# A hybrid encoder block on one core: attention's and gates' units as one matmul of 512 columns, evacuated by two engines

## The chip, the cores and the metric
The kernel runs on one core of a Trainium2 chip. The metric is the time of one execution on the device in microseconds; the median of three runs before the change is 1985.73 us (1985.63 to 1985.82).

## The reference, cut to what matters
One encoder layer on 256 tokens of width 2048, all in fp32:
```
xn   = rms_norm(x) * gain
cols = xn @ w_in      # q (16 heads of 128) | k, v (4 heads) | RWKV-7 columns | gate_attn | gate_rwkv
q, k = rope(q), rope(k)
o_attn = softmax(q k^T / sqrt(128), window 128, with a sink logit) @ v
merged = sigmoid(gate_attn) * o_attn + sigmoid(gate_rwkv) * o_rwkv
h = x + rms_norm(merged @ w_out)
h = h + rms_norm(relu(rms_norm(h) @ w_ffn_up)^2 @ w_ffn_down)
```
The change touches the projection of q, k, v and gate_attn alone.

## The kernel before
**Units.** Every weight matrix is streamed through SBUF in units of 1 MB: a unit is a block of 128 columns of w_in by all 2048 rows, as 16 tiles (k) of 128 x 128. SyncE loads it to a slot of `raw`. ScalarE rounds it to fp32r (`whi`, the high part), VectorE computes the rest (`wlo` = raw - whi). Tokens are held in the same way, turned: xT[:, k, 0, :] is high, xT[:, k, 1, :] low. whi and wlo have two buffers each and the banks PB[0] and PB[1] alternate by unit. A unit's product is high x high + high x low + low x high.

In `unit_b` this is three matmuls of 256 columns for each k, into columns 0 to 255 of the bank (lines 1586 to 1588). `unit_wide`, which the up projection of the feed-forward part uses (lines 1600 and 1602), and `dense` in the pair stage (lines 1766 and 1768) move the high and the low tokens together as 512 columns under the high weights, and then the high tokens under the low weights into columns 0 to 255; the result is the sum of the bank's two halves.

**Stages.** Units 0 to 23 are attention's: for each of four groups g a key, a value and four query units (steps j = 0 to 5). Units 24 to 39 are gates' (four, then a loop of three times four). Then come the RWKV-7 pairs, the output projection and the feed-forward part, to the end.

**Order by hand.** Each engine walks through the steps with its own `step` function, in a written order, and waits on semaphores. The four heads of group g are handled one step after another, shifted: within step j, the scores of head h have j = h + 3, the turn of its probabilities (transposes, line 1663) j = h + 4, and the product with the values (`weigh`, line 1672) j = h + 5, all modulo 6. So it is in every engine:
- TensorE, step of unit u: wait that unit u - 2 is evacuated (`d_evac`) and that this unit's low part is there (`w_lo`); the first four k, `weigh`, four more k; `scores` (line 1654, waits for the rotated query `q_r`); the last eight k (`w_used`); `turn` (waits for the normalised probabilities `prn`).
- ScalarE: `evacuate` after `w_used` (lines 493 to 495: the tokens, and the tokens with halves of 64 partitions exchanged, for the rotation; line 485 for values), the copy of an attention output to mrg (512), the copy of the turned probabilities to prT (507), the high part of unit u + 2 (477), the exponentials (521, wait for `neg`). For a gate, `gate_tanh` (502) from the bank takes the place of `evacuate`.
- VectorE: `maxima` (950 to 959, wait for `sc`), `rotate` (930, 931, 937, wait for `d_evac`) or, for a gate, `gate_product` (944), the low part of unit u + 2 (976; 872 in the gates' loop), `normalise` (964 to 969, wait for `ex`).

SyncE starts a load of attention when the low part of the unit three places earlier has been computed, in the gates with four slots.

## Time and profile before
| | |
|---|---|
| median of three runs | 1985.73 us |
| the profiled execution's own time | 1988.33 us |
| its span, first to last instruction | 1986.5 us |
| mean granted TensorE clock | 0.997 |
| TensorE busy | 1931.3 us |
| VectorE, ScalarE, GpSimd busy | 1357.8, 941.9, 379.1 us |
| bytes by DMA | 281.24 MB, 142 GB/s |

A row of a view in order of time has start and busy time in us, engine, line, operation, tiles written and read, and in brackets the idle time before it and what ended it. PE is TensorE's matmuls, PEld its weight loads, DVE VectorE, ACT ScalarE, POOL GpSimd. The ends of matmuls are modelled. A wait is put down to the signal that came last.

### The profile page before, as it was taken

The page shows a single profiled execution, that of the slowest core. Times are in us where ns is not written, and L with a number is a line of the kernel's source. Part 1 is how long each engine was busy: PE and PEld are TensorE (multiplying, and loading weights), DVE is VectorE, ACT ScalarE, POOL GpSimd, SP SyncE. Part 2 cuts the span into 40 slices and gives each one's busy share as a digit, 9 for nine tenths or more (in the row PEclk, how much of TensorE's full clock was granted, in tenths as well). Part 3 has the DMA queues.
Part 4 walks back from the last instruction along what each step waited for, and adds up shares of the span by engine and source line. Part 5 has one row for each costly group of instructions (what it writes and reads, how often), then busy time and mean ns, then how long its engine had stood idle before and what let it go on. Part 6 is the DMA issues. An engine that isn't in the chain of part 4 may idle for free.

```text
span 1986.5 us, 35360 instructions
## 1 busy us (share of the span) xinstructions
PE 1931.3 (97%) x12443; PEld 1720.7 (87%) x12443; DVE 1357.8 (68%) x2357; ACT 941.9 (47%) x1669; POOL 379.1 (19%) x451
## 2 busy tenths in 40 slices
PE   6999999999999999999999999999999999999997
PEld 6999999888888888888888888888888888888886
DVE  4666546888888888888888864656565655556565
ACT  5555434455454555545555544544443434444443
POOL 1000000444343333434344531100000000000001
PEclk9999999999999999999999999999999999999999
DMA  7455676433333333333331426456666665666663
GB/s 224 135 140 148 172 189 159 131 92 91 91 82 78 85 91 91 91 91 91 81 80 48 134 85 241 120 191 191 191 190 191 189 190 191 189 192 188 195 186 126
DMA packets 415373, 281.24 MB, mean 142 GB/s; under 512 B 14074, under 2 KB 372700, under 8 KB 414556
## 3 DMA queue, kind: packets, MB, share of 16 engines
q1 hardware_dynamic: 414908, 277.43, 48.3%
q10 hardware_dynamic: 416, 3.15, 0.4%
q8 instruction: 32, 0.52, 0.1%
q14 instruction: 17, 0.14, 0.0%
HBM read 278.46 MB, written 2.10 MB: 141 GB/s over the span
## 4 chain that ended last, share of the span: by engine, by line
PE 73%; issue 10%; DVE 9%; POOL 6%; ACT 1%; DMA 0%; DVEq 0%; POOLq 0%; SPq 0%; ACTq 0%
PE bank L1600 12%; PE bank L1602 6%; PE bank L1766 6%; PE bank L1616 6%; PE bank L1617 6%; PE bank L1618 6%; PE bank L1586 4%; PE bank L1588 4%; PE bank L1587 4%; POOL CT L1513 3%; DVE wlo L872 3%; PE bank L1768 3%; PE bank L1895 2%; PE bank L1913 1%; PE bank L1745 1%
## 5 line engine op out<-in xcount | busy, mean ns | idle before, releaser
L1766 PE MATMUL bank<-xT,whi 128*128 128x512 f32 x1024 | 318.0, 418 | 0.0
L872 DVE TENSOR_TENSOR wlo<-raw,whi 128x1024 fp32r<-128x1024 f32 (+2 forms) x181 | 259.1, 1438 | 47.7 <-ACT whi L449 43.6
L1403 DVE TENSOR_TENSOR wlo<-raw,whi 128x1024 fp32r<-128x1024 f32 x126 | 154.4, 1225 | 163.0 <-ACT whi L834 158.8
L1600 PE MATMUL bank<-xT,whi 128*128 128x512 f32 x1024 | 245.7, 391 | 0.0
L834 ACT ACTIVATE whi<-raw 128x1024 fp32r<-128x1024 f32 x126 | 133.1, 1056 | 206.1 <-PE bank L1618 206.1
L1600 PEld LDWEIGHTS bank<-xT,whi 128*128 128x128 f32 x1024 | 188.1, 188 | 36.2
L1586 PE MATMUL bank<-xT,whi 128*128 128x256 f32 x736 | 216.6, 294 | 0.6 <-DVE wlo L872 0.6
L1588 PE MATMUL bank<-xT,wlo 128*128 128x256 f32 x736 | 207.9, 283 | 0.0
L1587 PE MATMUL bank<-xT,whi 128*128 128x256 f32 x736 | 207.9, 283 | 0.0
L1616 PE MATMUL bank<-whi,ft 128*128 128x512 f32 x512 | 199.3, 389 | 0.0
L1617 PE MATMUL bank<-wlo,ft 128*128 128x512 f32 x512 | 199.3, 389 | 0.0
L1618 PE MATMUL bank<-whi,ft 128*128 128x512 f32 x512 | 199.2, 389 | 0.0
L441 ACT ACTIVATE whi<-raw 128x1024 fp32r<-128x1024 f32 x190 | 198.9, 1047 | 0.0
L1768 PEld LDWEIGHTS bank<-xT,wlo 128*128 128x128 f32 x1024 | 167.3, 188 | 28.8
L1766 PEld LDWEIGHTS bank<-xT,whi 128*128 128x128 f32 x1024 | 171.2, 191 | 16.8 <-issue 0.3
L1768 PE MATMUL bank<-xT,wlo 128*128 128x256 f32 x1024 | 176.0, 280 | 0.0
L1513 POOL TENSOR_TENSOR CT<-G,lmk 128x256 fp32r<-128x256 f32 x192 | 145.0, 760 | 75.6 <-PE bank L1895 74.3
L1410 DVE TENSOR_TENSOR wlo<-raw,whi 128x1024 fp32r<-128x1024 f32 x126 | 153.5, 1218 | 0.0
L1570 POOL TENSOR_TENSOR acc<-acc,gain 128x512 f32<-128x512 f32 x6 | 8.8, 1487 | 703.0 <-ACT junk L818 703.0
L1586 PEld LDWEIGHTS bank<-xT,whi 128*128 128x128 f32 x736 | 140.7, 191 | 1.6 <-issue 0.7
L1587 PEld LDWEIGHTS bank<-xT,whi 128*128 128x128 f32 x736 | 140.8, 191 | 0.9
L1588 PEld LDWEIGHTS bank<-xT,wlo 128*128 128x128 f32 x736 | 140.7, 191 | 0.0
(234 smaller groups left out, 3833.2 us busy)
## 6 DMA issues: line engine op xcount, KB each, us to landing
raw<-in_w_in SPq DMA_DIRECT2D x106, 1024.0 KB, 6.0
raw<-in_w_ffn_up SPq DMA_DIRECT2D x64, 1024.0 KB, 6.4
raw<-in_w_ffn_down SPq DMA_DIRECT2D x64, 1024.0 KB, 5.0
raw<-in_w_out SPq DMA_DIRECT2D x16, 1024.0 KB, 5.6
raw<-in_w_in SPq DMA_DIRECT2D x4, 768.0 KB, 4.6
xtok<-in_x SPq DMA_DIRECT2D x2, 1024.0 KB, 6.1
upg<-in_g_up SPq DMA_DIRECT2D x16, 128.0 KB, 3.4
hres<-in_x ACTq DMA_DIRECT2D x1, 2048.0 KB, 10.8
```

Source lines behind the costliest of these rows:

```text
L441: A.activation(whi[:, u_static % 2, 1024:], raw[:, u_static % 4, 1024:], ACT.Copy).then_inc(w_hi.sem, 1)
L872: x = V.tensor_tensor(wlo[:, u_static % 2, part], raw[:, u_static % 4, part], whi[:, u_static % 2, part].bitcast(f32), ALU.subtract)
L1513: Gp.tensor_tensor(in_blocks(CT[c][:].rearrange("p a b -> p (a b)"), l), woven(G[:, 0, :, :, :], l, 2 * c, 2), in_blocks(lmk[:, l, :, :].r ...
L1586: M(bank[:, 0:T], h, xT[:, k, 0, :], start=k == 0, stop=False)
L1587: M(bank[:, 0:T], h, xT[:, k, 1, :], start=False, stop=False)
L1588: x = M(bank[:, 0:T], l, xT[:, k, 0, :], start=False, stop=k == KT - 1)
L1600: M(bank[:, :], hi[:, P * k:P * k + P], xT[:, k, :, :], start=k == 0, stop=False)
L1616: M(banks[b][:, :], ah, wh, start=f, stop=False)
L1617: M(banks[b][:, :], ah, wl, start=False, stop=False)
L1618: x = M(banks[b][:, :], al, wh, start=False, stop=e)
L1766: M(bank[:, :], hi[:, P * k:P * k + P], xT[:, k, :, :], start=k == 0, stop=False)
L1768: x = M(bank[:, 0:T], lo[:, P * k:P * k + P], xT[:, k, 0, :], start=False, stop=k == KT - 1)
```

## The change
Attention's and gates' units call `unit_wide` in place of `unit_b`. Their result now lies in both halves of the bank. ScalarE copies the half of the high weights with the low tokens (columns 256 to 511) to SBUF and raises a new semaphore, `tok`; VectorE then adds the other half in place (`join`) and raises `d_evac`, which ScalarE raised before. In attention, ScalarE then makes the exchanged halves out of the sum, from SBUF (`swap_halves`), behind the copies of mrg, prT and vtok; for a gate, it applies tanh in place. On VectorE, `join` stands first in every step, ahead of `maxima`. The low-rank units of the RWKV part keep `unit_b`.

```diff
--- before.py
+++ after.py
@@ -258,7 +258,7 @@
             k_r1=1, k_r=1, v_tp=1, v_tok=1, q_r1=4, q_r=4, sc=4, sc_m=4, mx=4, mx2=4, neg=4,
             ex=4, esink=4, den=4, rden=4, prn=4, p_tp=4, p_T=4, pv=4, o_ev=4,
 
-            ga_m=4, lo_nb=1, lo_df=1, lo_sh=1, lo_act=1, lo_fin=1, drv=1, zr=1, d_cp=4,
+            ga_m=4, tok=1, lo_nb=1, lo_df=1, lo_sh=1, lo_act=1, lo_fin=1, drv=1, zr=1, d_cp=4,
 
             up_ld=1, sh_nb=1, sh_df=1, shifted=1, gate_t=1, sqd=1, ss=1, ssm=1, rs=1, rrep=1, rbc=1, nkk=1, gg=2,
             kAB=1, rkd=1, lw=1, la=1, lg=1, tws=1, decs=2, tas=1, gups=1, scan=2, inv=2, ar=2, tt=2, bhs=2, km1=2, km2=2,
@@ -298,6 +298,12 @@
             if isinstance(n, int) and n == 0:
                 return U_RW0 + j, U_RW0 + j
             return U_RW + j, 4 * n + U_RW + j
+
+        def tok_step(j, g):
+
+            if g is None:
+                return 11 * KVH + 2 * j
+            return 11 * g + (0, 2, 3, 5, 7, 9)[j]
 
         def raw_count(u_static):
 
@@ -479,27 +485,35 @@
             def evacuate(j, g, u_static, u):
 
                 act.wait_ge(w_used.sem, w_used.n(u + 1))
-                bank = PB[u_static % 2]
                 if j == 1:
                     act.wait_ge(s["v_tp"].sem, s["v_tp"].before(g))
-                    A.activation(vf[:], bank[:, 0:T], ACT.Copy).then_inc(d_evac.sem, 1)
-                    return
-
-                if j == 0:
-                    act.wait_ge(s["q_r1"].sem, s["q_r1"].before(g))
+                    dst = vf[:]
                 else:
-                    act.wait_ge(s["k_r1"].sem, s["k_r1"].at(g))
-                    act.wait_ge(s["q_r1"].sem, s["q_r1"].at(g, j - 2))
-                A.activation(tokA[:, 0, :], bank[:, 0:T], ACT.Copy)
-                A.activation(tokA[0:64, 1, :], bank[64:P, 0:T], ACT.Copy)
-                A.activation(tokA[64:P, 1, :], bank[0:64, 0:T], ACT.Copy).then_inc(d_evac.sem, 1)
-
-            def gate_tanh(j, i):
+                    if j == 0:
+                        act.wait_ge(s["q_r1"].sem, s["q_r1"].before(g))
+                    else:
+                        act.wait_ge(s["k_r1"].sem, s["k_r1"].at(g))
+                        act.wait_ge(s["q_r1"].sem, s["q_r1"].at(g, j - 2))
+                    dst = tokA[:, 0, :]
+                A.activation(dst, PB[u_static % 2][:, T:2 * T], ACT.Copy).then_inc(s["tok"].sem, 1)
+
+            def swap_halves(u):
+
+                act.wait_ge(d_evac.sem, d_evac.n(u + 1))
+                A.activation(tokA[0:64, 1, :], tokA[64:P, 0, :], ACT.Copy)
+                A.activation(tokA[64:P, 1, :], tokA[0:64, 0, :], ACT.Copy).then_inc(s["tok"].sem, 1)
+
+            def gate_half(j, i):
 
                 u = U_GA + j
                 act.wait_ge(w_used.sem, w_used.n(4 * i + u + 1))
-                act.wait_ge(s["ga_m"].sem, s["ga_m"].at(i, j))
-                A.activation(tokA[:, j % 2, :], PB[u % 2][:, 0:T], ACT.Tanh, scale=0.5).then_inc(d_evac.sem, 1)
+                act.wait_ge(s["ga_m"].sem, s["ga_m"].at(i, j - 1) if j else s["ga_m"].before(i))
+                A.activation(tokA[:, j % 2, :], PB[u % 2][:, T:2 * T], ACT.Copy).then_inc(s["tok"].sem, 1)
+
+            def gate_tanh(j, i):
+
+                act.wait_ge(d_evac.sem, d_evac.n(4 * i + U_GA + j + 1))
+                A.activation(tokA[:, j % 2, :], tokA[:, j % 2, :], ACT.Tanh, scale=0.5).then_inc(s["tok"].sem, 1)
 
             def turned(g, h):
 
@@ -527,7 +541,7 @@
 
                 u = u_static + 6 * i
                 if g is None:
-                    gate_tanh(j, 0)
+                    gate_half(j, 0)
                 else:
                     evacuate(j, g, u_static, u)
                 h = (j + 1) % 6
@@ -539,6 +553,10 @@
                 if j == 2 and g is not None:
                     act.wait_ge(s["v_tp"].sem, s["v_tp"].at(g))
                     A.activation(vtok[:].rearrange("p a b -> p (a b)"), PB[2][:, 0:T], ACT.Copy).then_inc(s["v_tok"].sem, 1)
+                if g is None:
+                    gate_tanh(j, 0)
+                elif j != 1:
+                    swap_halves(u)
                 cut_attention(u_static + 2, i)
                 h = (j + 3) % 6
                 if hg is not None and h < 4:
@@ -560,11 +578,13 @@
                 step(j, KVH - 1, KVH - 1, 18 + j)
             for j in (0, 1, 2):
                 step(j, None, KVH - 1, U_GA + j)
+            gate_half(3, 0)
             gate_tanh(3, 0)
             cut_hi(U_GA + 5, U_GA + 5)
 
             with act.Fori(0, 3, 1) as i:
                 for j in range(4):
+                    gate_half(j, i + 1)
                     gate_tanh(j, i + 1)
                     cut_hi(U_GA + j + 2, 4 * i + 4 + U_GA + j + 2)
 
@@ -916,6 +936,17 @@
             dve.wait_ge(s["ld_c2"].sem, s["ld_c2"].n(32))
             cos, sin = csa[:, CA_COS:CA_COS + T], csa[:, CA_SIN:CA_SIN + T]
             wmask = csa[:, CA_MASK:CA_MASK + 2 * T]
+            def join(j, g, u_static, u, i=0):
+
+                bank = PB[u_static % 2]
+                if g is None:
+                    dve.wait_ge(s["tok"].sem, s["tok"].n(tok_step(j, None) + 8 * i + 1))
+                    dst = tokA[:, j % 2, :]
+                else:
+                    dve.wait_ge(s["tok"].sem, s["tok"].n(tok_step(j, g) + 1))
+                    dst = vf[:] if j == 1 else tokA[:, 0, :]
+                V.tensor_tensor(dst, dst, bank[:, 0:T], ALU.add).then_inc(d_evac.sem, 1)
+
             def rotate(j, g):
 
                 r1, r2 = (s["k_r1"], s["k_r"]) if j == 0 else (s["q_r1"], s["q_r"])
@@ -938,7 +969,7 @@
 
             def gate_product(j, i):
 
-                dve.wait_ge(d_evac.sem, d_evac.n(4 * i + U_GA + j + 1))
+                dve.wait_ge(s["tok"].sem, s["tok"].n(tok_step(j, None) + 8 * i + 2))
                 dve.wait_ge(s["o_ev"].sem, s["o_ev"].n(4 if isinstance(i, int) else 16))
                 m = mrg[:, bass.ds(j + 4 * i, 1), :].rearrange("p a t -> p (a t)")
                 V.scalar_tensor_tensor(m, tokA[:, j % 2, :], 1.0, m, ALU.add, ALU.mult).then_inc(s["ga_m"].sem, 1)
@@ -979,13 +1010,14 @@
             def step(j, g, hg, u_static, i=0):
 
                 u = u_static + 6 * i
+                join(j, g, u_static, u)
                 h = (j + 3) % 6
                 if hg is not None and h < 4:
                     maxima(hg, h)
                 if g is None:
                     gate_product(j, 0)
                 elif j != 1:
-                    dve.wait_ge(d_evac.sem, d_evac.n(u + 1))
+                    dve.wait_ge(s["tok"].sem, s["tok"].n(tok_step(j, g) + 2))
                     rotate(j, g)
                 cut_attention(u_static + 2, i)
                 if hg is not None and h < 4:
@@ -1002,11 +1034,13 @@
                 step(j, KVH - 1, KVH - 1, 18 + j)
             for j in (0, 1, 2):
                 step(j, None, KVH - 1, U_GA + j)
+            join(3, None, U_GA + 3, U_GA + 3)
             gate_product(3, 0)
             cut_lo(U_GA + 5, U_GA + 5)
 
             with dve.Fori(0, 3, 1) as i:
                 for j in range(4):
+                    join(j, None, U_GA + j, 4 * i + 4 + U_GA + j, i + 1)
                     gate_product(j, i + 1)
                     cut_lo(U_GA + j + 2, 4 * i + 4 + U_GA + j + 2)
 
@@ -1679,11 +1713,11 @@
                     pe.wait_ge(d_evac.sem, d_evac.n(u - 1))
                 h = (j + 1) % 6
                 if hg is not None and h < 4:
-                    unit_b(u_static, u, 0, 4)
+                    unit_wide(u_static, u, 0, 4)
                     weigh(hg, h)
-                    unit_b(u_static, u, 4, 8)
+                    unit_wide(u_static, u, 4, 8)
                 else:
-                    unit_b(u_static, u, 0, 8)
+                    unit_wide(u_static, u, 0, 8)
                 if j == 2 and g is not None:
                     pe.wait_ge(d_evac.sem, d_evac.n(u))
                     for tb in range(2):
@@ -1692,12 +1726,12 @@
                 h = (j + 3) % 6
                 if hg is not None and h < 4:
                     scores(hg, h)
-                unit_b(u_static, u, 8, KT)
+                unit_wide(u_static, u, 8, KT)
                 h = (j + 2) % 6
                 if hg is not None and h < 4:
                     turn(hg, h)
 
-            token_tiles(xtok, PB[2:6], "x_n", "x_lo", "x_tp", 0, 0, unit_b)
+            token_tiles(xtok, PB[2:6], "x_n", "x_lo", "x_tp", 0, 0, unit_wide)
             for j in (1, 2):
                 step(j, 0, None, j)
             with pe.Fori(0, KVH - 1, 1) as i:
@@ -1710,12 +1744,12 @@
             for j in (0, 1, 2):
                 step(j, None, KVH - 1, U_GA + j)
             pe.wait_ge(d_evac.sem, d_evac.n(U_GA + 2))
-            unit_b(U_GA + 3, U_GA + 3)
+            unit_wide(U_GA + 3, U_GA + 3)
 
             with pe.Fori(0, 3, 1) as i:
                 for j in range(4):
                     pe.wait_ge(d_evac.sem, d_evac.n(4 * i + 4 + U_GA + j - 1))
-                    unit_b(U_GA + j, 4 * i + 4 + U_GA + j)
+                    unit_wide(U_GA + j, 4 * i + 4 + U_GA + j)
             def low_rank(j):
 
                 pe.wait_ge(d_evac.sem, d_evac.n(U_LO + j - 1))
```

## Rows read from the trace of the kernel before

**Rows 1.** The page: busy us, share of the span and instructions by engine
```profile
PE 1931.3 (97%) x12443; PEld 1720.7 (87%) x12443; DVE 1357.8 (68%) x2357; ACT 941.9 (47%) x1669; POOL 379.1 (19%) x451
```

**Rows 2.** Windows: start:end, length, busy us by engine, clock, DMA share, GB/s
```profile
100.40:145.80 45.40, 44.37 (x339) 42.75 (x338) 30.26 (x58) 25.04 (x52) 0.00 (x0) 1.00 0.51 138
...
230.00:299.50 69.50, 69.50 (x581) 69.50 (x580) 32.62 (x24) 26.20 (x24) 0.00 (x0) 1.00 0.68 182
```

**Rows 3.** Waits of TensorE from 191 to 230 us: total, times, longest
```profile
PE bank L1672 <- ACT prT L507: 0.3, 1, 0.3
```

**Rows 4.** TensorE in order of time, last gate unit and first pair unit
```profile
299.40 0.28 PE L1588 MATMUL bank<-xT,wlo 128*128 128x256 f32 x1
299.52 3.82 PE L1766 MATMUL bank<-xT,whi 128*128 128x512 f32 x16
...
305.08 0.63 PE L1766 MATMUL bank<-xT,whi 128*128 128x512 f32 x2
```

**Rows 5.** ScalarE in order of time, one attention step (start, busy us)
```profile
112.19 0.38 ACT L493 ACTIVATE tokA<-bank 128x256 f32<-128x256 f32 x1 [3.75 <-PE bank L1588]
...
113.66 0.59 ACT L507 ACTIVATE prT<-bank 128x512 f32<-128x512 f32 x1
114.14 1.91 ACT L477 ACTIVATE whi<-raw 128x2048 fp32r<-128x2048 f32 x1
```

**Rows 6.** VectorE in order of time, two attention steps
```profile
103.31 0.69 DVE L950 TENSOR_TENSOR scm<-bank,csa 128x512 f32<-128x512 f32 x1
...
105.33 0.42 DVE L930 TENSOR_TENSOR tokB<-tokA,csa 128x256 f32<-128x256 f32 x1
...
113.39 0.42 DVE L930 TENSOR_TENSOR tokB<-tokA,csa 128x256 f32<-128x256 f32 x1 [0.75 <-ACT tokA L495]
...
114.18 0.43 DVE L937 TENSOR_TENSOR qr<-tokB 128x256 f32<-128x256 f32 x1
116.08 2.29 DVE L976 TENSOR_TENSOR wlo<-raw,whi 128x2048 fp32r<-128x2048 f32 x1 [1.47 <-ACT whi L477]
...
118.68 0.62 DVE L969 TENSOR_SCALAR prb<-prb,sm 128x256 f32<-128x256 f32 x2
```

**Rows 7.** ScalarE and VectorE in order of time, a pair's add and shift
```profile
708.86 0.38 ACT L585 ACTIVATE raw<-bank 128x256 f32<-128x256 f32 x1
...
709.27 0.42 DVE L1043 TENSOR_TENSOR raw<-raw,bank 128x256 f32<-128x256 f32 x1 [0.94 <-ACT raw L585]
709.61 0.95 DVE L1065 SCALAR_TENSOR_TENSOR nb<-nb,raw 128x768 f32<-128x768 f32 x1
...
710.72 1.28 DVE L1071 SCALAR_TENSOR_TENSOR sh<-nb,pA,raw 128x256 f32<-128x256 f32 x3 [0.16 <-DVE nb L1065]
...
712.13 0.51 ACT L640 ACTIVATE nb<-sh,pB 128x256 f32<-128x256 f32 x1 [0.21 <-DVE sh L1071]
```

**Rows 8.** All engines in order of time, scores that wait for a query
```profile
144.58 0.42 DVE L937 TENSOR_TENSOR qr<-tokB 128x256 f32<-128x256 f32 x1
...
145.06 0.73 PEld L1654 LDWEIGHTS bank<-kr,qr 128*128 128x128 f32 x4 [0.15 <-DVE qr L937]
```

**Rows 9.** TensorE in order of time, from turn over weigh to scores
```profile
111.91 0.60 PE L1663 MATMUL bank<-cst,prb 128*128 128x128 f32 x4
112.27 0.36 PE L1586 MATMUL bank<-xT,whi 128*128 128x256 f32 x1
...
114.30 1.13 PE L1672 MATMUL bank<-prT,vtok 128*128 128x256 f32 x4 [0.37 <-ACT prT L507]
...
116.70 1.02 PE L1654 MATMUL bank<-kr,qr 128*128 128x256 f32 x4
```

**Rows 10.** ScalarE's first evacuation and TensorE's unit 2 in order of time
```profile
33.05 0.38 ACT L493 ACTIVATE tokA<-bank 128x256 f32<-128x256 f32 x1 [2.04 <-PE bank L1588]
...
38.62 0.36 PE L1586 MATMUL bank<-xT,whi 128*128 128x256 f32 x1
```

**Rows 11.** Lines of ScalarE, by form: busy us, mean ns, idle before
```profile
L695 ACT ACTIVATE TS<-DT 128x256 fp32r<-128x256 f32 x160 | 67.0, 419 | 19.4 <-DVE DT L1220 18.3
```

## The prediction

> **What bounds the kernel now.** I read the page first: TensorE is busy 97% of the span, VectorE 68%, ScalarE 47% [rows 1]. The windows by stage then show where TensorE is not full: a group of six attention units takes 45.4 us and leaves TensorE idle 1.0 us; in the 12 gate units between 230 and 299.5 us it is never idle; the granted clock is 1.00, its 2.4 GHz level, in both [rows 2]. So in the gates every nanosecond of matmul counts, and in attention both matmuls and waits do. The view of waits names the waits of TensorE in attention: on prT, ScalarE's copy of the turned probabilities (line 507); in the last group, where gates begin, little of it is left [rows 3]. The view gives only idle time after the matmuls have drained; spacings of matmuls tell the true loss, so I work with those.
>
> **The matmuls.** The last gate unit and the first pair unit stand side by side: narrow matmuls start every 0.12 us, three to a k, so a unit takes 48 x 0.12 = 5.76 us; the wide unit runs from 299.52 to 305.08, 5.56 us [rows 4]. A changed unit saves 0.20 us. Forty change (24 attention, 16 gate): 8.0 us, if nothing takes it back. Only one weight load in three goes, and it was mostly hidden; the columns stay the same.
> The Trainium skill, "TensorE: Matmul & The Clock Gate", section "Back-to-back issue gap", gives 262 cycles for 256 columns and 518 for 512; by that, an estimate from its table, a unit would save only 16 x 6 cycles at 2.4 GHz, 0.04 us. The row of the trace has five times that, and the sum goes by the row.
>
> **The evacuation.** Call E the modelled end of a unit's last matmul; ScalarE starts 0.11 us later (its copy starts at 112.19, E is 112.08). Before, in attention, ScalarE does three copies (1.19 us with their gaps) and that of mrg (0.28), so that it reaches prT 1.47 after the first, and then cuts the high part of the weights, 1.91 [rows 5]. VectorE begins the maxima (lines 950 to 959) as soon as it has normalised, 0.4 to 1.6 us before E, since the scores come in the middle of a unit; then it rotates, cuts the low part and normalises [rows 6].
> After, ScalarE makes one copy (E+0.11 to E+0.49), VectorE adds, ScalarE swaps the halves. The add exists in the pair units as line 1043: it starts 0.03 us after ScalarE's copy, lasts 0.42 and lets the next start after 0.34. From VectorE's end to ScalarE's start it is 0.13 (712.00 to 712.13) [rows 7]; from ScalarE to VectorE 0.03, and I take 0.10, between them and near the first. The join thus runs from E+0.52 to E+0.94. VectorE is free by then: it ends normalising at 119.30, ahead of the next E.
> The important edit is the order: join stands ahead of maxima on VectorE. In the four steps of a group that have maxima, these can't start before E any more; they start at E+0.85, take 2.02 to the rotation (103.31 to 105.33), and the rotation takes 1.22 [rows 6], so the rotated query comes at E+4.09 and TensorE has it at E+4.15 (0.06 after VectorE's end, 145.00 to 145.06 [rows 8]). Queued behind the rotation are the low cut and normalise; TensorE's scores and turn wait for them.
>
> **When TensorE wants it.** Its next slot is at E-0.16. Half a unit now takes 2.78. A turn of the probabilities takes 0.36 (111.91 to 112.27), and a unit's first matmul after it 0.07 more than its 0.12. Between the weigh's start and the scores lie 2.40, of which twelve matmuls are 1.44; that leaves 0.96 for a weigh that waited and for the first matmul behind it, 0.86 where it did not [rows 9].
> - Scores of head 0 (after the step without maxima): two half copies follow the join, E+1.04 to E+1.82, rotation until E+3.07, TensorE E+3.13; it asks at about E+2.68 (half a unit, 0.06 of pause). Wait 0.45, with a restart of some 0.07.
> - Scores of head 1: no turn or weigh ahead, asked for at E+2.68, there at E+4.15: wait 1.47. Before, this was 0.11 [rows 8].
> - Heads 2 and 3: turn and weigh ahead, asked at E-0.16+0.36+0.07+2.78+0.86, E+3.9: wait 0.25 each.
> - Turn of head 3: the step in front has maxima, the low cut starts at E+4.01 when the rotation lets it, and with normalise takes 3.22 (116.08 to 119.30 [rows 6]), TensorE has it at E+7.29; the unit after it has no scores, so TensorE asks at E-0.16+0.36+0.07+5.56+0.86, E+6.69: wait 0.60.
> Sum 3.02, plus about 0.37 for restarts of the matmul stream (0.1 each where it did not wait before): 3.39 us a group.
> What goes: prT was late because of the three copies. The weigh at 114.30 had its slot at 113.78 (0.12 after the last matmul), loss 0.52, the middle of the group's three (0.44 to 0.54); with 0.08 of restart each 1.74 us [rows 5, 9]. Now ScalarE reaches prT at E+0.56 to E+0.67, TensorE could start at E+1.40 to E+1.51 and asks at E-0.16+0.36+0.07+1.39, E+1.66: no wait, with 0.14 to spare. The old 0.11 goes too. With six units' 1.20: 3.05 us gained a group.
> Net per group in the loop (three of them): +0.34, together +1.0 us. In the last group, three of whose steps are gates, prT cost less: 0.3 idle once [rows 3], about 0.7 with what the idle view leaves out. It has no late turn, since a gate's product (0.43) is shorter than a rotation: -1.20 - 0.7 - 0.11 against waits of 0.52 + 1.47 + 0.25 + 0.25 with 0.2 of restarts, less some 0.3 because its unrolled steps wait less for addresses: +0.4.
>
> **Start.** Unit 2's weights wait for the evacuation of unit 0, whose E is 32.94, 0.11 before ScalarE's copy. With two more links (join, swap at E+1.04, high cut from E+1.84, low cut from E+3.78) they are ready at E+6.13, 39.07, or 0.15 sooner with the faster unit 0; unit 2 started at 38.62. It starts 0.3 later and gives 0.2 back: +0.1 [rows 10].
>
> **Gates.** The chain to the weights of the next unit but one: copy from E+0.11, join until E+0.94, tanh at E+1.04, cut of the high part 0.3 later (a tanh that reads SBUF, priced by line 695: 0.42 [rows 11]), 1.91 of it [rows 5], then 0.03 and the low cut's 2.29 [rows 6]: E+5.58, TensorE at E+5.64. Its slot without a wait is E-0.16+5.56 = E+5.40. It waits about 0.24 at every second unit: (5.56 + 5.80)/2 = 5.68 a unit against 5.76. Thirteen units: -1.0 us. Loads ahead: SP waits for w_lo three units back, and the queue moves 182 GB/s at a share of 0.68 [rows 2], so a megabyte is here in time for a unit a little shorter.
>
> **Sum.** +1.0 +0.4 +0.1 -1.0 = +0.5 us. The profiled execution (1988.33 with a span of 1986.5) would become 1988.8; the median shown, 1985.73, is 2.6 lower than that execution, so 1986.2. An 8 us saving goes into waits.
>
> **Bounds.** The join: between 0.34 (its spacing in line 1043) and 0.43 (a third of line 1071's 1.28 [rows 7]). Each 0.1 of delay of the join comes back in five waits of four groups, 2.0 us, and half of it in 13 gate units, 0.65; the latencies between the two engines (0.03 to 0.13) could be 0.05 to 0.1 off in sum: -2 to +3 us. The swap reads SBUF: up to 0.42 [rows 11] instead of 0.40 each, 0.2 us in all. Restarts: nothing to twice the size, -1.5 to +1.5.
>
> **Rivals.**
> 1. Forecast: gains and new waits cancel; 1982.5 to 1990.5. 0.66.
> 2. Faster: scores don't wait, because VectorE's work behind the join overlaps more than the rows show, or prT's release feeds on. If the waits for queries halve, 4 x 1.2 = 5 us less: 1981.5; if none came, some 12 less, 1974. Against it: maxima follow join in one queue. 0.12.
> 3. Slower: the join is late, by VectorE still normalising or ScalarE's wait for it. From 0.15 us of lateness it costs 4 us; at 0.3 it is 8 us, and prT (0.14 to spare) does not suffer, being ahead of the swap: 1990 to 1995. 0.17.
> 4. The wide unit saves nothing in attention, where it runs in blocks of four or eight k between other matmuls: 0.20 x 27 = 5.4 us come back, little in the gates, which wait anyway: 1991.8. Against it: the spacings are TensorE's own [rows 4], and nothing in a short block changes them. 0.05. The section of the Trainium skill's page on TensorE named above leans to this side.
> Measured to about 0.2%, 4 us: faster 0.12, same 0.68, slower 0.20. Range 1981.5 to 1991.5.
>
> **What would show it.** Groups of 45 to 46 us as before (TensorE idle some 2.5 us in them, against 1.0); waits of TensorE on qr of some 1.5 us once a group and 0.3 to 0.5 three times, one on prb of 0.6; none on prT. VectorE's maxima after the join. Gate units in pairs of about 5.6 and 5.8 us, TensorE waiting for wlo. Pair and feed-forward stages unchanged. I am wrong if a group takes under 44.5 or over 47 us, or a gate unit over 5.8.

## The result, and the profile after

The changed kernel takes 1990.78 us (median of 12 runs), the kernel before 1986.70 in the same runs; the ratio is 1.0019, 95% interval 1.0012 to 1.0027. That is 3.8 us slower by the ratio and 4.1 by the medians, at the edge of what counted as no change (4 us), where 0.5 us had been forecast. The runs of either kernel lie in two bunches of six about 2 us apart, and bunch against bunch the changed kernel is 3.9 and 4.3 us slower. The profiled span is 1989.8 us against 1986.5, at the same mean granted clock, 0.997.

The page of the changed kernel, busy us by engine, answers to [rows 1]: TensorE does 640 matmuls fewer and is busy 3.7 us less, over a span 3.3 us longer.

```profile
PE 1927.6 (97%) x11803; PEld 1687.6 (85%) x11803; DVE 1373.2 (69%) x2397; ACT 951.4 (48%) x1685; POOL 379.3 (19%) x451
```

Where the time went is read best from one event that each unit has in both traces, the start of ScalarE's evacuation of it. Unit 0's differs by up to 1.3 us among all the traces of this study, even where nothing up to there differs (31.75 in e6, 32.99 in e7), so I count from it.

| unit evacuated | before, us | after, us | difference | added since the line above |
|---|---|---|---|---|
| 0 | 33.05 | 32.40 | -0.65 | |
| 2 | 44.85 | 44.70 | -0.15 | +0.50 start |
| 8 | 90.30 | 91.03 | +0.73 | +0.88 first group |
| 14 | 135.70 | 137.46 | +1.76 | +1.03 second group |
| 20 | 181.05 | 183.90 | +2.85 | +1.09 third group |
| 26 | 224.84 | 228.50 | +3.66 | +0.81 last group |
| 39 | 299.80 | 302.85 | +3.05 | -0.61 gates |
| 40 (first pair unit) | 305.42 | 308.81 | +3.39 | +0.34 |

At unit 42 it is still 3.40, and the spans differ by 3.3: the pair and feed-forward stages give nothing and take nothing. Everything is decided in the first 310 us, where the last column sums to +4.04 (unit 0 itself came 0.65 earlier, which makes 3.39).

The waits of TensorE in the changed kernel from 20 to 330 us (total, times, longest) answer to [rows 3]:

```profile
PE bank L1688 <- DVE qr L968: 6.0, 6, 1.5
PE bank L1688 <- issue: 1.8, 2, 1.2
PE bank L1697 <- DVE prb L1000: 1.5, 3, 0.5
PE bank L1634 <- DVE wlo L1007: 0.7, 1, 0.7
```

No wait for prT is left (3.4 us in ten waits before); scores (line 1688) wait for the rotated query and the turn (1697) for the normalised probabilities, as forecast; waits of about 0.2 us don't show as idle time here, since the last matmul's modelled end covers them. "Issue" in the second row is the same wait in the last group, where no releaser was found. The fourth row is unit 2, whose weights come late at the start.

### The profile page after: what moved, and what is told of

It reads as the page before. It is cut to its first block, busy times and chain, and to the rows that moved or that the text cites. A ratio compares the mean times of both kernels' runs of the same rounds, so it can differ in the third digit from the quotient of the medians.

```text
span 1989.8 us, 34173 instructions
## 1 busy us (share of the span) xinstructions
PE 1927.6 (97%) x11803; PEld 1687.6 (85%) x11803; DVE 1373.2 (69%) x2397; ACT 951.4 (48%) x1685; POOL 379.3 (19%) x451
## 4 chain that ended last, share of the span: by engine, by line
PE 70%; issue 11%; DVE 10%; POOL 6%; ACT 2%; DMA 0%; DVEq 0%; POOLq 0%; ACTq 0%; SPq 0%
PE bank L1634 17%; PE bank L1636 9%; PE bank L1800 6%; PE bank L1650 6%; PE bank L1652 6%; PE bank L1651 6%; POOL CT L1547 3%; DVE wlo L892 3%; PE bank L1802 3%; PE bank L1929 2%; PE bank L1947 1%; PE bank L1779 1%; PE bank L1952 1%; PE bank L1781 1%; PE bank L1780 1%
## 5 line engine op out<-in xcount | busy, mean ns | idle before, releaser
L1634 PE MATMUL bank<-xT,whi 128*128 128x512 f32 x1664 | 416.4, 397 | 0.8 <-DVE wlo L1007 0.7
L1634 PEld LDWEIGHTS bank<-xT,whi 128*128 128x128 f32 x1664 | 304.4, 188 | 59.8 <-DVE wlo L892 1.2
L1800 PE MATMUL bank<-xT,whi 128*128 128x512 f32 x1024 | 317.9, 418 | 0.1
L1636 PEld LDWEIGHTS bank<-xT,wlo 128*128 128x128 f32 x1664 | 220.7, 191 | 13.0
L1636 PE MATMUL bank<-xT,wlo 128*128 128x256 f32 x1664 | 224.4, 282 | 0.0
L1802 PEld LDWEIGHTS bank<-xT,wlo 128*128 128x128 f32 x1024 | 167.4, 188 | 28.6
L1800 PEld LDWEIGHTS bank<-xT,whi 128*128 128x128 f32 x1024 | 171.2, 191 | 17.1 <-issue 0.6
L1802 PE MATMUL bank<-xT,wlo 128*128 128x256 f32 x1024 | 175.9, 280 | 0.0
L1254 DVE TENSOR_TENSOR DT<-DT,bank 128x256 fp32r<-128x256 f32 x192 | 79.8, 417 | 63.6 <-PE bank L1947 60.2
L718 ACT ACTIVATE W<-bank 128x256 fp32r<-128x256 f32 x192 | 73.6, 383 | 89.6 <-PE bank L1929 89.6
L862 ACT ACTIVATE fa<-bank 128x256 f32<-128x256 f32 x64 | 24.6, 384 | 187.1 <-PE bank L1636 187.1
L1652 PEld LDWEIGHTS bank<-whi,ft 128*128 128x128 f32 x512 | 96.1, 188 | 20.0
```

The source lines that it names most:

```text
L1634: M(bank[:, :], hi[:, P * k:P * k + P], xT[:, k, :, :], start=k == 0, stop=False)
L1636: x = M(bank[:, 0:T], lo[:, P * k:P * k + P], xT[:, k, 0, :], start=False, stop=k == KT - 1)
L1652: x = M(banks[b][:, :], al, wh, start=False, stop=e)
L1800: M(bank[:, :], hi[:, P * k:P * k + P], xT[:, k, :, :], start=k == 0, stop=False)
L1802: x = M(bank[:, 0:T], lo[:, P * k:P * k + P], xT[:, k, 0, :], start=False, stop=k == KT - 1)
```

## The chain, link by link

ScalarE and VectorE in order of time in the step that is followed by the scores of head 1. The unit's modelled end E is 98.23, by the 0.11 of the forecast. A "slot" below is the moment at which TensorE would have started something had it not waited.

```profile
98.34 0.38 ACT L498 ACTIVATE tokA<-bank 128x256 f32<-128x256 f32 x1 [3.57 <-PE bank L1636]
99.22 0.42 ACT L503 ACTIVATE tokA<-tokA 64x256 f32<-64x256 f32 x1 [0.49 <-DVE tokA L948]
99.64 0.42 ACT L504 ACTIVATE tokA<-tokA 64x256 f32<-64x256 f32 x1
100.09 1.91 ACT L483 ACTIVATE whi<-raw 128x2048 fp32r<-128x2048 f32 x1
```
```profile
98.76 0.42 DVE L948 TENSOR_TENSOR tokA<-tokA,bank 128x256 f32<-128x256 f32 x1 [1.66 <-ACT tokA L498]
99.10 0.68 DVE L981 TENSOR_TENSOR scm<-bank,csa 128x512 f32<-128x512 f32 x1
...
101.17 0.43 DVE L961 TENSOR_TENSOR tokB<-tokA,csa 128x256 f32<-128x256 f32 x1
...
101.97 0.43 DVE L968 TENSOR_TENSOR qr<-tokB 128x256 f32<-128x256 f32 x1
102.31 2.29 DVE L1007 TENSOR_TENSOR wlo<-raw,whi 128x2048 fp32r<-128x2048 f32 x1
```

The join runs from E+0.53 to E+0.95 (forecast 0.52 to 0.94), the rotation starts at E+2.94 (2.87), ends at E+4.17 (4.09). TensorE around it, and in the step with turn and weigh that answers to [rows 9]:

```profile
100.66 0.28 PE L1636 MATMUL bank<-xT,wlo 128*128 128x256 f32 x1
102.45 1.13 PE L1688 MATMUL bank<-kr,qr 128*128 128x256 f32 x4 [1.51 <-DVE qr L968]
...
114.30 0.60 PE L1697 MATMUL bank<-cst,prb 128*128 128x128 f32 x4
114.66 1.17 PE L1634 MATMUL bank<-xT,whi 128*128 128x512 f32 x4
115.66 0.62 PE L1636 MATMUL bank<-xT,wlo 128*128 128x256 f32 x4
116.12 1.02 PE L1706 MATMUL bank<-prT,vtok 128*128 128x256 f32 x4
116.79 1.28 PE L1634 MATMUL bank<-xT,whi 128*128 128x512 f32 x4
117.91 0.64 PE L1636 MATMUL bank<-xT,wlo 128*128 128x256 f32 x4
118.62 0.48 PE L1688 MATMUL bank<-kr,qr 128*128 128x256 f32 x1
```

The last matmul ahead of the second scores starts at 100.66, so their slot, 0.12 later, was 100.78: they wait 1.67 us. The weigh (116.12) follows its unit's matmuls without a wait, where before it lost 0.52 [rows 9].

The gates, in order of time: TensorE first (one row of x16 is a unit's high weights, the next its low weights), then ScalarE and VectorE.

```profile
274.07 3.82 PE L1634 MATMUL bank<-xT,whi 128*128 128x512 f32 x16
277.72 2.07 PE L1636 MATMUL bank<-xT,wlo 128*128 128x256 f32 x16
279.82 0.98 PE L1634 MATMUL bank<-xT,whi 128*128 128x512 f32 x3
```
```profile
274.35 0.39 ACT L511 ACTIVATE tokA<-bank 128x256 f32<-128x256 f32 x1 [2.88 <-PE bank L1636]
275.22 0.42 ACT L516 ACTIVATE tokA<-tokA 128x256 f32<-128x256 f32 x1 [0.49 <-DVE tokA L948]
275.54 1.90 ACT L455 ACTIVATE whi<-raw 128x2048 fp32r<-128x2048 f32 x1
279.91 0.38 ACT L511 ACTIVATE tokA<-bank 128x256 f32<-128x256 f32 x1 [2.47 <-PE bank L1636]
...
285.81 0.39 ACT L511 ACTIVATE tokA<-bank 128x256 f32<-128x256 f32 x1 [2.80 <-PE bank L1636]
```
```profile
277.48 2.29 DVE L892 TENSOR_TENSOR wlo<-raw,whi 128x2048 fp32r<-128x2048 f32 x1 [1.26 <-ACT whi L455]
```

The low cut ends at 279.77 and TensorE starts the unit but one at 279.82, 5.58 us after E (274.24); its slot was 279.63 (274.07 + 5.56). The units are 5.56 and 5.90 us long in turn (279.91 - 274.35, 285.81 - 279.91).

## The experiments

Below, "from unit 0 to 40" is the change of that stretch against the kernel before, "a group" that of one turn of the attention loop (units 10 to 16), "gates" that of units 27 to 39, each by evacuation starts as in the table above. For the changed kernel they are +4.04, +1.04 and -0.42 us. There is one trace for each kernel; stretches that two kernels share agree within some 0.05 us.

One thing has to be taken out before the figures are compared: a short stretch at the lower level of TensorE's clock. In the kernel before it lies at 1262 us, behind a wait of 2.18 us; 32 matmuls of line 1638 take 5.44 us there, and in e4 the same 32, behind the same wait, take 3.81. The windows show a mean granted clock of 0.59 there (part of it at the 1.2 GHz level), and 1.00 (2.4 GHz) in e4.

```profile
1261.14 5.44 PE L1638 MATMUL bank<-diag,hres 128*128 128x128 f32 x32 [2.18 <-DVE diag L900]
1262.00:1266.00 4.00, 4.00 (x24) 4.00 (x24) 2.90 (x5) 1.96 (x5) 0.00 (x0) 0.59 0.20 49
```
```profile
1262.28 3.81 PE L1672 MATMUL bank<-diag,hres 128*128 128x128 f32 x32 [2.18 <-DVE diag L920]
```

It costs 1.6 us. The traces of before, changed, e3 and e7 have it at that place, that of e8 at 56 us, inside the first group, behind a wait of 2.03 us; the other seven have none ahead of the program's last 10 us. So the difference between before and changed is free of it, the stretches up to unit 40 are free of it in all but e8, and a comparison of spans or medians is not.

| kernel | ratio to before, 95% interval | unit 0 to 40 | a group | gates |
|---|---|---|---|---|
| changed | 1.0019 (1.0012 to 1.0027) | +4.04 | +1.04 | -0.42 |
| e1 | 1.0038 (1.0024 to 1.0052) | +7.87 | +1.90 | -0.57 |
| e2 | 1.0038 (1.0024 to 1.0052) | +6.84 | +1.41 | +0.43 |
| e3 | 0.9997 (0.9988 to 1.0006) | -0.81 | -0.01 | -0.62 |
| e4 | 1.0006 (0.9997 to 1.0015) | +1.96 | +1.02 | -2.10 |
| e5 | 0.9985 (0.9976 to 0.9994) | -2.67 | -0.01 | -2.11 |
| e6 | 0.9999 (0.9990 to 1.0009) | -0.01 | +0.11 | -0.42 |
| e7 | 1.0005 (0.9996 to 1.0014) | +1.18 | +0.87 | -2.10 |
| e8 | 1.0054 (1.0038 to 1.0069) | +11.62 (1.6 of it the clock) | +2.63 | 0.00 |
| e9 | 0.9984 (0.9975 to 0.9993) | -3.04 | -0.14 | -2.11 |
| e10 | 0.9965 (0.9951 to 0.9978) | -5.12 | -0.59 | -2.32 |

**e1: the maxima ahead of the join.**
```diff
-                join(j, g, u_static, u)
                 h = (j + 3) % 6
                 if hg is not None and h < 4:
                     maxima(hg, h)
+                join(j, g, u_static, u)
```


> The changed kernel with one swap on VectorE: in every step the maxima come ahead of the join, as they came ahead of the rotation before. Theory A (the order is what costs: the join in front holds up the maxima, these the rotation, this the scores): the waits for the second, third and fourth scores of a group fall from 1.68, 0.22 and 0.23 us to under 1, 0 and 0; each group about 1.2 us shorter than the 46.4 of the changed kernel, the whole about 5 us faster than it, some 1 us faster than before. Theory B (the length of the chain copy, add, swap, high cut, low cut, normalise costs, wherever the maxima stand): the maxima can't start before the normalising behind the low cut has ended, near the unit's end, so they now hold up the join, the swap and the cuts behind it; the second scores wait about 0.9 us, but third and fourth 0.4 each and all four turns 0.2 to 1.5; a group 47 to 48 us, the whole 4 to 6 us slower than the changed kernel, 1994 to 1997. My walk by the rows gives B.

Measured: 0.9 us a group slower than the changed kernel (47.3 us), 3.8 in all, a little under the 4 to 6 of theory B. VectorE in order of time:

```profile
105.27 0.62 DVE L1000 TENSOR_SCALAR prb<-prb,sm 128x256 f32<-128x256 f32 x2
105.80 0.68 DVE L981 TENSOR_TENSOR scm<-bank,csa 128x512 f32<-128x512 f32 x1
...
107.82 0.42 DVE L948 TENSOR_TENSOR tokA<-tokA,bank 128x256 f32<-128x256 f32 x1
109.14 0.43 DVE L961 TENSOR_TENSOR tokB<-tokA,csa 128x256 f32<-128x256 f32 x1 [0.91 <-ACT tokA L504]
...
111.08 2.29 DVE L1007 TENSOR_TENSOR wlo<-raw,whi 128x2048 fp32r<-128x2048 f32 x1 [0.72 <-ACT whi L483]
```

The maxima start the moment the normalising ends, and the join stands behind them, so that the exchange, both cuts and the next normalising come later. The waits of TensorE show the trade:

```profile
PE bank L1688 <- DVE qr L968: 5.1, 12, 0.9
PE bank L1697 <- DVE prb L1000: 4.6, 4, 1.3
```

Theory A's cure is refuted: with the longer evacuation, either order costs. B had the direction and the cost at the turns.

**e2: narrow matmuls, evacuation and order of the engines as changed.**
```diff
-                    M(bank[:, :], hi[:, P * k:P * k + P], xT[:, k, :, :], ...)
...
+                    M(bank[:, 0:T], hi[:, P * k:P * k + P], xT[:, k, 0, :], ...)
+                    M(bank[:, T:2 * T], hi[:, P * k:P * k + P], xT[:, k, 1, :], ...)
```


> The changed kernel with its evacuation and its order, but three matmuls of 256 columns for each k in place of one of 512 and one of 256; the product of high weights and low tokens goes to the other half of the bank. It isolates what the matmul's form gives. Theory: 0.20 us a unit in TensorE's stream (5.76 against 5.56), of which the waits that follow the unit's end hide none but those half a unit later hide half: 0.6 us a group, 0.2 for each unit at the start, 0.05 a gate unit, 4 us in all slower than the changed kernel, 7.5 slower than before: about 1994. Rival: TensorE is bound by the waits alone and the form gives nothing: the time of the changed kernel. Second rival: the form saves less in short blocks than in a whole unit: groups 0.3 us longer or less.

Measured: +2.80 against the changed kernel where 4 was expected; 0.37 a group rather than 0.6, 0.85 in the gates' twelve units rather than 0.6. The form gives something everywhere, but in attention only a third of the 1.2 us of six units. The reason offered, that a unit that ends sooner asks sooner for what other engines make, fits the waits: from e2 to the changed kernel those for queries grow from 7.1 to 7.8 us between 20 and 330 us, those for probabilities from 1.1 to 1.5. The edit also takes each k's low product right behind its high ones, where `unit_wide` does all high ones first. That this matters isn't seen in the spacings: matmuls of 256 columns start 0.12 us apart in either order.

**e3: only the gates changed** (attention's `evacuate`, `unit_b` and order from the kernel before).
```diff
+                unit = unit_wide if g is None else unit_b
```


> Only the gates' 16 units are wide with their new evacuation; attention's 24 units, their copies and their order are those of before. Theory: the loss of the changed kernel is all in attention: groups of 45.4 us as before, three gate units inside the last group 0.15 to 0.2 faster each, thirteen at 5.73 against 5.76, one step of 0.3 slower at the end: 0.5 to 1 us faster than before, 3.5 to 4 faster than the changed kernel. Rival: the gates' chain costs as well, in that the add ahead of the maxima holds up the last head: no faster than before, or slower.

Measured: -0.81, too little for the ratio to tell; groups unchanged to 0.01 us. The loss is attention's alone: +4.04 - (-0.81) = 4.85 us.

**e4: tanh behind the high cut, product behind the low cut, in the last 13 gates.**
```diff
                     gate_half(j, i + 1)
-                    gate_tanh(j, i + 1)
                     cut_hi(U_GA + j + 2, 4 * i + 4 + U_GA + j + 2)
+                    gate_tanh(j, i + 1)
...
-                    gate_product(j, i + 1)
                     cut_lo(U_GA + j + 2, 4 * i + 4 + U_GA + j + 2)
+                    gate_product(j, i + 1)
```


> The changed kernel with the last 13 gates reordered: on ScalarE the tanh stands behind the high cut, on VectorE the product behind the low cut. Attention untouched. Theory (the gate units are bound by the chain copy, add, tanh, high cut, low cut, 5.58 us from the unit's end): without add and tanh the chain is 4.7 us, no wait for weights is left, every gate unit takes 5.56 us in place of 5.56 and 5.90 in turn: 2.2 us faster than the changed kernel. Rival: the 5.90 is TensorE's own (a restart after the evacuation's wait, or the bank): no change.

Measured: -2.08 against the changed kernel, with TensorE's units in the loop all 5.56 to 5.57 us from start to start (ScalarE in order of time):

```profile
273.12 0.39 ACT L511 ACTIVATE tokA<-bank 128x256 f32<-128x256 f32 x1 [3.16 <-PE bank L1636]
273.40 1.91 ACT L455 ACTIVATE whi<-raw 128x2048 fp32r<-128x2048 f32 x1
275.20 0.41 ACT L516 ACTIVATE tokA<-tokA 128x256 f32<-128x256 f32 x1
278.69 0.39 ACT L511 ACTIVATE tokA<-bank 128x256 f32<-128x256 f32 x1 [3.08 <-PE bank L1636]
```

The 5.90 was the chain, not TensorE by itself.

**e5: e3 and e4's order together.**

> Attention as before, the 16 gate units wide with their new evacuation, and the last 13 of them with the tanh behind the high cut and the product behind the low cut: the two parts of which the one was measured at 0.8 us and the other at 2.0. Theory (the parts add, since the chain of the gates has nothing to do with attention's): gate units of 5.56 us, 2.8 us faster than before, about 1984.5 where before has 1987.4. Rival: the three gates with heads beside them lose something when TensorE reaches them sooner: 2 us or less.

Measured: -2.67, ratio 0.9985 (0.9976 to 0.9994): faster than both kernels. The parts (-0.81 and -2.08) add to within 0.2 us.

**e6: without the exchange of halves.**
```diff
-                A.activation(tokA[0:64, 1, :], tokA[64:P, 0, :], ACT.Copy)
-                A.activation(tokA[64:P, 1, :], tokA[0:64, 0, :], ACT.Copy).then_inc(s["tok"].sem, 1)
+                act.sem_inc(s["tok"].sem, 1)
...
-                V.tensor_tensor(tokB[:, 1, :], tokA[:, 1, :], sin, ALU.mult).then_inc(r1.sem, 1)
+                V.tensor_tensor(tokB[:, 1, :], tokA[:, 0, :], sin, ALU.mult).then_inc(r1.sem, 1)
```


> The changed kernel without the two copies that exchange the halves (the rotation reads the sum twice, so keys and queries are not rotated rightly). It takes ScalarE's 0.86 us and the signal to and fro out of the chain. Theory: only the first scores of a group wait for the swap (their step has no maxima); that wait of 0.73 us and its restart go, the three others stay, since there VectorE is at the maxima while ScalarE swaps; the turn of the last head stays too: a group 45.5 to 45.7 us against 46.4, in all some 3.5 us faster than the changed kernel, the time of before. Rival (the swap is what makes the chain long everywhere): all waits shrink by 0.8 us, a group 2 us shorter, 4 us faster than before.

Measured: 0.93 us a group less than the changed kernel, 4.05 in all, as forecast ("the time of before"); unit 2's wait at the start is gone too. Of the waits for queries the three long ones of the loop stay (and one as "issue" in the last group); the first scores' is gone:

```profile
PE bank L1687 <- DVE qr L967: 4.5, 3, 1.5
PE bank L1696 <- DVE prb L999: 1.3, 3, 0.4
PE bank L1687 <- issue: 1.2, 1, 1.2
```

The exchange on SBUF costs its step about as much as the whole loss of a group. The rival (the exchange lengthens every wait) is not borne out: the wait of 1.5 us stands.

**e7: rotation between the parts of the maxima, and e4's order.**
```diff
-                    maxima(hg, h)
+                    masked(hg, h)
...
                     rotate(j, g)
+                if hg is not None and h < 4:
+                    maxima(hg, h)
```


> The changed kernel with the maxima split on VectorE: join, add of the mask to the scores (0.72 us, in the time in which ScalarE swaps), rotation, and then the rest of the maxima (1.3 us); gates reordered as in the fourth run (2.0 us). If the rotation's place behind the whole maxima is what costs: queries are there at about 3.2 us after the unit's end in place of 4.2, the second scores' wait falls from 1.68 to 0.6, the third and fourth vanish, the turn of the last head waits 0.3 more (its low cut starts later): 1.1 to 1.4 us a group less than 46.4, in all 5 us less in attention and 2 in the gates: 3 us faster than before, about 1984.5. Rival: low cut and normalise, later by 0.3, hold up all four turns, and the gain is under 0.5 us a group.

Measured: a miss. 0.17 us a group less than the changed kernel, not 1.1 to 1.4; the rival was right. The kernel is 1.2 us slower than before, not 3 faster, and 2.1 of what it regained is the gates'. VectorE's order and TensorE's waits:

```profile
106.58 0.42 DVE L948 TENSOR_TENSOR tokA<-tokA,bank 128x256 f32<-128x256 f32 x1
106.92 0.68 DVE L981 TENSOR_TENSOR scm<-bank,csa 128x512 f32<-128x512 f32 x1
108.74 0.43 DVE L961 TENSOR_TENSOR tokB<-tokA,csa 128x256 f32<-128x256 f32 x1 [1.13 <-ACT tokA L504]
...
111.17 2.29 DVE L1010 TENSOR_TENSOR wlo<-raw,whi 128x2048 fp32r<-128x2048 f32 x1
```
```profile
PE bank L1702 <- DVE prb L1003: 4.8, 7, 0.9
PE bank L1693 <- DVE qr L968: 3.3, 6, 0.6
```

The second scores wait 0.6 as forecast, but VectorE stands idle 0.5 to 1.1 us for the exchange, which in the step shown, the worst of the group, stands behind ScalarE's copy of prT. The low cut starts at E+5.1 there, at E+4.0 in the same step of the changed kernel; in the other steps it is 0.4 to 0.6 later (0.3 had been expected). The turns wait 4.8 us where the changed kernel had 1.5.

**e8: the kernel before, maxima held until the unit is evacuated.**
```diff
                 if hg is not None and h < 4:
+                    dve.wait_ge(d_evac.sem, d_evac.n(u + 1))
                     maxima(hg, h)
```


> The kernel before with one added wait: VectorE starts the maxima only when the unit has been evacuated, which is what the join in front of them does in the changed kernel. Three matmuls of 256 columns, three copies by ScalarE, no add. Theory (this order is the price): the copies end 1.29 us after the unit's end, maxima until 3.35, rotation until 4.55; the second scores wait some 1.9 us, the turn of the last head some 0.3, the others 0 to 0.2: 2.2 us a group, 8 to 9 us slower than before. Rival: the price of the changed kernel comes from its add and swap, and the order alone costs under 1 us a group.

Measured: 2.63 us a group, somewhat over the forecast's 2.2. In all it is 11.6, of which 1.6 is the stretch at the lower clock in the first group (that one is +4.23): 10.0 against a forecast of 8 to 9. Holding up the maxima alone costs more than the whole change. They are held longer here than in the changed kernel (they start at E+1.50 in place of E+0.87), so the figure isn't the price of its order. prT's waits stay, since the three copies do. The window of the lower clock, and the waits:

```profile
56.00:59.60 3.60, 3.60 (x14) 3.31 (x15) 2.90 (x5) 0.00 (x0) 0.00 (x0) 0.53 0.03 8
```
```profile
PE bank L1655 <- DVE qr L937: 6.0, 3, 2.0
PE bank L1673 <- ACT prT L507: 3.4, 10, 0.4
```

**e9: e5 and wide value units.**
```diff
-                unit = unit_wide if g is None else unit_b
+                unit = unit_wide if g is None or j == 1 else unit_b
```


> The fifth kernel, and attention's four value units wide too, with copy and join. Values aren't rotated and their step has no maxima, so the longer evacuation has nothing behind it but the high cut, which ScalarE does without waiting for the join. Theory: 0.2 us for each of the four units, of which the turn of the last head, which follows that unit, may take back up to 0.2 where it has no slack: 0.4 to 0.8 us less than the fifth kernel by the trace, too little for the times to tell. Rival: the join on VectorE ahead of the low cut holds it up: no gain.

Measured: 0.37 us less than e5 by the trace, 0.13 a group, and no difference in the ratio (0.9984): just under the 0.4 to 0.8 expected.

**e10: the kernel before with wide matmuls and its old evacuation of the first half.**
```diff
-                    unit_b(u_static, u, 0, 4)
+                    unit_wide(u_static, u, 0, 4)
```


> The kernel before with wide matmuls in attention and gates and nothing else: ScalarE evacuates as before, and the half of the bank with high weights times low tokens is left out of the result. It gives the wide form without its evacuation. Theory (the 8.0 us of the form are there, and are lost in the longer evacuation): gates 0.20 a unit, 2.6 us in thirteen; in attention 1.2 us a group less what comes back as waits of some 0.1 each for prT, queries and turns, whose makers are no faster: 0.7 to 0.9 a group; start 0.4: 6 to 7 us faster than before. Rival: TensorE in attention is bound by its waits, so that a shorter unit gives next to nothing there: 3 us faster.

Measured: -5.12 us by the trace (0.59 a group, 2.32 in twelve gate units). The gates give the full 0.19 a unit, a group half of its 1.20: more than the rival's 3, less than the 6 to 7 expected. The ratio, 0.9965, would be 7 us. But all five runs of e10 have the mean granted clock 0.998, twelve of the fifteen of the kernel before 0.997. Against the other three, its median of 1980.5 is 5.2 us less than their 1985.7, as the trace says.

Against e10, the changed kernel's evacuation and order cost 1.63 us a group net (1.04 + 0.59). The exchange from SBUF accounts for 0.93 of it by e6; the 0.7 left, for the join and its place, was not taken apart.

## Why the prediction came out as it did

The range (1981.5 to 1991.5) held the time, 1990.78, with 0.7 us to spare, and "no change" was called with 0.68. That owes something to luck: the waits that the prediction named are there, but all four terms of the sum erred to the same side, and the sum was 3.5 us too low, +0.5 forecast against +4.04 by the trace from unit 0 to 40. The time lies above the 1982.5 to 1990.5 of the forecast's own rival and inside the 1990 to 1995 of "slower". One of the signs of being wrong was met, a gate unit over 5.8 (every second takes 5.90); the group, 46.4, is above the 45 to 46 forecast and under the 47 of the sign, with TensorE idle 2.7 us in it (2.5 forecast). Term by term:

- **The form, 0.20 us a unit**: right (5.56 in the gates once nothing waits, e4). That 8.0 us are fully there is not: with no longer evacuation at all they are 5.1 (e10). In the forecast, a shorter unit brought TensorE's requests forward only where it counted slots.
- **prT's waits gone, 1.74 us a group**: right; no such wait is left, and the step in front of the values' evacuation became 0.82 us shorter (0.62 and 0.20).
- **New waits, 3.02 us a group: mis-sized.** The waits for scores: 0.73 for the first (at 94.22, slot 93.49; 0.45 forecast), 1.67 for the second (1.47), 0.2 for the third and fourth (0.25), the last turn 0.67 (at 129.95, slot 129.28; 0.60). For the first, the exchange is later by 0.10: it starts at E+1.07 behind the copy of vtok, not at E+1.04, and a copy of 64 partitions from SBUF takes 0.42 with the next 0.43 behind it, where 0.40 each was taken. Its matmuls then start 0.12 after the rotation's end (94.10), not 0.06. For the second, the rotation ends 0.08 late. For both, TensorE asks 0.11 to 0.13 us sooner than I had it, since I counted a pause of 0.06 and the old position of E (the next unit starts at E-0.25 here, not E-0.16). A group is +1.0 instead of +0.34, of which the waits are 0.5; the other 0.2 was not taken apart. That is 2.0 us of the miss in three groups, and 0.4 more in the last group.
- **Gates, -1.0: a size.** The chain is 5.58 (5.64 forecast) and the wait 0.19; but the unit behind a wait takes 5.72, not 5.56 (279.82 to 285.54, where the next one starts): a restart of 0.16 that the sum had charged in attention and not here. Mean 5.73 instead of 5.68; and the last of these waits falls to the first pair unit, +0.34. Together -0.27.
- **Start, +0.1: measured +0.50.** The forecast's figure has 0.15 for a faster unit 0 in it, which lies ahead of the point that I count from, so like for like it is +0.25. Unit 2 started at 38.60, 6.31 after E (6.13 forecast): 0.09 for the same slower exchange, and 0.15 from the low cut's end (38.45) to TensorE where 0.06 was taken.
- **The order as the cause** ("the important edit is the order"): the experiments make this narrower. Held-up maxima do cost, 2.6 us a group in a kernel with nothing else changed (e8, where they are held longer). But the changed kernel can't be mended by putting them first (e1, 0.9 worse) nor by taking the rotation out from behind them (e7, 0.17 better). The cause is a loop: copy, join, exchange, high cut, low cut, normalise, and the next turn. In each order tried, the link that was set back held up something that TensorE waits for: the queries in the changed kernel, the turns in e7, both in e1. What the change adds to the loop is one round from ScalarE to VectorE and back and two copies that were there before and are now behind it; without those two copies attention up to unit 26 is within 0.3 us of the old time (e6). What the join alone costs no run shows.
- **The rivals**: "slower by a late join" named the right side, and a time that came out, for the wrong link: the join was within 0.01 us of its forecast. "Nothing in short blocks" is not borne out: e2 gives 0.37 a group to the form.

By the table of the Trainium skill, "TensorE: Matmul & The Clock Gate", section "Back-to-back issue gap", the prediction had estimated a saving of 0.04 us a unit. The runs don't agree with it: gate units of 5.76 became 5.56.

Left open: why e2 gives 0.37 a group and e10 0.59. Their waits differ: between 20 and 330 us those for queries and probabilities grow by 1.1 us from e2 to the changed kernel, those for prT by 0.2 from before to e10 (3.4 to 3.6), which was not taken apart by group. Open is also what decides where the stretch at the lower clock falls, since e4 has the same wait of 2.18 us without it. That stretch is what parts the late stages of the traces: the spans of e1, e2 and e4, which have none, are 1.6 to 1.7 us shorter than their places at unit 42 say.

## What to carry to other kernels

A cheaper form of an operation moves the point at which its engine asks for everything else; before counting the gain, walk along the round trip that the new form needs, from the unit's end through each engine's queue to the next request, and see how many requests lie behind it. Split such a change by stage: here the wide form pays where only one short chain hangs on the evacuation (gates, 0.2 us a unit once tanh and product stand behind the cuts) and not where a rotation and a softmax are queued behind it. When TensorE starts again after a wait, its next unit is longer as well (here by 0.16 us): charge the restart with the wait. And before comparing two spans, look at the granted clock by window: one short stretch at the lower level is worth as much as many an edit.

## What the runs showed that was not expected

- After a wait of only 0.19 us, the 32 matmuls of a gate unit take 5.72 us instead of 5.56; the restart costs about as much as the wait.
- Two 64-partition copies from SBUF to shifted partitions take 0.42 us each and start 0.43 apart (lines 503 and 504 above); from a bank they took 0.38 and started 0.39 apart in the kernel before (lines 494 and 495, at 33.44 and 33.83).
- From VectorE's end to ScalarE's start it is 0.03 us where ScalarE stands waiting (the join ends at 275.19, tanh starts at 275.22), as little as the other way, where 0.13 had been read from [rows 7].
- A stretch at the 1.2 GHz level that costs 1.6 us comes and goes between traces of kernels that are equal in that place, and in e8 it fell into the first group, where it looked like a part of the edit's price.
